# Attention of a two-block network: the value products of a pair in one turn instead of two

## The reference

```python
def gqa_attend(q, k, v):
    bsz, nq, _, _ = q.shape
    qg = q.reshape(bsz, nq, KV_HEADS, ATT_HEADS // KV_HEADS, HEAD_DIM)
    s = jnp.einsum('bqhgd,bkhd->bhgqk', qg, k).astype(jnp.float32) * HEAD_DIM ** -0.5
    p = jax.nn.softmax(s, axis=-1).astype(v.dtype)
    o = jnp.einsum('bhgqk,bkhd->bqhgd', p, v)
    return o.reshape(bsz, nq, ATT_HEADS * HEAD_DIM)
...
    k_all = jnp.concatenate([kc, kx], axis=1)
    v_all = jnp.concatenate([vc, vx], axis=1)
    o_x = lax.map(lambda qb: gqa_attend(qb, k_all, v_all), q_blocks)
    y_x = o_x.swapaxes(0, 1).reshape(bsz, n, nq) @ w_out
```

## Time and profile before

| | |
|---|---|
| median of 3 runs | 2515.29 us (2514.77 to 2516.95) |
| profiled execution: span from first to last instruction | 2512.5 us; the median lies 2.8 us above it, and no other time of this execution is given |
| PE busy | 2491.2 us, 99% |
| DVE busy | 1611.4 us, 64% |
| ACT busy | 972.5 us, 39% |
| mean granted TensorE clock | 0.998 |

### The profile page before, as it was taken

One profiled execution on the slowest core, in us unless ns is written; L12 is line 12 of the kernel. 1 busy time (PEld: TensorE's weight loads), 2 busy tenths in 40 slices (PEclk: granted clock), 3 DMA queues, 4 the chain that ended last, 5 costly groups with the idle time before them and its releaser, 6 DMA issues.

```text
span 2512.5 us, 36307 instructions
## 1 busy us (share of the span) xinstructions
PE 2491.2 (99%) x14058; PEld 2125.8 (85%) x14058; DVE 1611.4 (64%) x2551; ACT 972.5 (39%) x1483; POOL 117.9 (5%) x211
## 2 busy tenths in 40 slices
PE   8999999999999999999999999999999999999998
PEld 6888888888888888779888888898888888888887
DVE  5777667665546567766655575776667777644446
ACT  6243533131313245764332244353232454533224
POOL 0000000100000000000000000010001000000000
PEclk9999999999999999999999999999999999999999
DMA  7323314433333321002545553224546323132222
GB/s 288 120 99 110 127 50 143 159 118 110 114 110 134 110 76 51 2 1 93 199 152 169 173 192 113 101 88 172 187 158 219 135 95 110 68 101 93 100 96 97
DMA packets 83965, 303.70 MB, mean 121 GB/s; under 512 B 9200, under 2 KB 11376, under 8 KB 83568
## 3 DMA queue, kind: packets, MB, share of 16 engines
q1 hardware_dynamic: 58336, 208.92, 24.0%
q0 software_dynamic: 25488, 92.81, 10.8%
HBM read 299.60 MB, written 2.10 MB: 120 GB/s over the span
## 4 chain that ended last, share of the span: by engine, by line
PE 96%; DMA 2%; DVE 1%; issue 0%; ACT 0%; SPq 0%; POOL 0%; POOLq 0%; ACTq 0%; DVEq 0%
PE G L648 20%; PE G L650 20%; PE G L649 20%; PE G L675 5%; PE G L676 5%; PE G L677 5%; PE G L742 2%; PE G L743 2%; PE G L744 2%; PE B L1243 2%; PE G L827 1%; DMA Araw<-adaw_dram 1%; PE G L829 1%; PE G L828 1%; PE B L1219 1%; PE G L1203 1%
## 5 line engine op out<-in xcount | busy, mean ns | idle before, releaser
L1391 ACT ACTIVATE Whi<-Wraw 128x1024 fp32r<-128x1024 f32 x333 | 349.6, 1051 | 411.4 <-DMA Wraw<-wstream_dram 399.3
L2038 DVE TENSOR_TENSOR Wlo<-Wraw,Whi 128x1024 fp32r<-128x1024 f32 x333 | 406.9, 1222 | 116.4 <-ACT Whi L1391 115.2
L648 PE MATMUL G<-hs_hi,Whi 128*128 128x512 f32 x672 | 264.2, 393 | 0.0
L650 PE MATMUL G<-hs_hi,Wlo 128*128 128x512 f32 x672 | 261.6, 389 | 0.0
L649 PE MATMUL G<-hs_lo,Whi 128*128 128x512 f32 x672 | 261.5, 389 | 0.0
L2053 DVE SCALAR_TENSOR_TENSOR Araw<-Araw,CB 128x1024 f32<-128x1024 f32 x176 | 214.3, 1220 | 20.6 <-DMA Araw<-adaw_dram 20.5
L2113 DVE SCALAR_TENSOR_TENSOR X<-G,MOD,X 128x256 f32<-128x256 f32 (+1 forms) x104 | 65.2, 655 | 206.0 <-PE G L650 154.9
L594 POOL DMA_DIRECT2D Araw<-adaw_dram x176 | 93.2, 530 | 1692.4 <-DVE Araw L2053 1637.9
L648 PE MATMUL G<-h_lat_hi,Whi 128*128 128x512 f32 x424 | 165.7, 391 | 0.0
L649 PE MATMUL G<-h_lat_lo,Whi 128*128 128x512 f32 x424 | 165.1, 389 | 0.0
L650 PE MATMUL G<-h_lat_hi,Wlo 128*128 128x512 f32 x424 | 165.1, 389 | 0.0
(11 more groups left out here) (636 smaller groups left out, 6169.5 us busy)
## 6 DMA issues: line engine op xcount, KB each, us to landing
Wraw<-wstream_dram SPq DMA_DIRECT2D x333, 512.0 KB, 3.3
Araw<-adaw_dram POOLq DMA_DIRECT2D x176, 512.0 KB, 3.8
Eraw<-wstream_dram SPq DMA_DIRECT2D x22, 512.0 KB, 4.4
FIRST<-firstw_dram SPq DMA_DIRECT2D x6, 1024.0 KB, 18.7
X<-xin_dram SPq DMA_DIRECT2D x4, 768.0 KB, 7.0
X<-xin_dram SPq DMA_DIRECT2D x2, 1536.0 KB, 7.3
out_dram<-X SPq DMA_DIRECT2D x16, 128.0 KB, 1.7
ROW<-rows_dram SPq DMA_DIRECT2D x2, 768.0 KB, 6.5
```

Of the source, the lines that this page charges most:

```text
L648: pe.matmul(o, wh, hi[:, a:b], start=(k == 0), stop=False)
L650: last = pe.matmul(o, wl, hi[:, a:b], start=False, stop=(k == kt - 1))
L1391: act.activation(hi, raw, ACT.Copy).then_inc(w_hi, 1)
L2038: dve.tensor_tensor(lo, raw, hi.bitcast(F32), ALU.subtract).then_inc(w_lo, 1)
```

## The change

PE's list in the attention is written in another order. In even turns from 2 on all six key tiles are done for the pair; odd turns have no values; the exception of the last turn is gone. ACT's and DVE's lists stay as they are, and so do all waits.

```diff
@@ -1268,8 +1268,7 @@
             scores_of(0)
             latent_values(1, 2, 3, 4)
             for n in range(2 * AH):
-                r, i0 = n // 2 - 1, 3 * (n % 2)
-                last_pair = n + 1 == 2 * AH
+                r = n // 2 - 1
                 if n == 2:
                     pe.wait_ge(qk_std, 4)
                     pe.wait_ge(at_used_act, 3)
@@ -1280,12 +1279,10 @@
                     latent_values(7)
                 for part in range(3):
                     turn_probs(n, part)
-                    if last_pair and part == 0:
-                        attend(r, i0)
                 if n == 0:
                     latent_values(5, 6)
-                if r >= 0:
-                    for i in range(i0 + 1 if last_pair else i0, i0 + 3):
+                if r >= 0 and n % 2 == 0:
+                    for i in range(TT):
                         attend(r, i)
                 if n % 4 == 0 and n > 0:
                     spread_sums(n // 4 - 1)
```

## The result

The changed kernel takes 2532.45 us (median of 5 runs, 2530.26 to 2532.91), the kernel before 2514.77 us beside it (5 runs, 2512.66 to 2516.95): 17.7 us more, ratio 1.007, 95% interval 1.0059 to 1.008. The forecast was 2533.5 us, 18.2 us more than the 2515.3 us known then.

A forecast was written before the change was run, and what follows sets the result against it. PE was taken to bound the kernel, with the chain on it for 96% of the span. 20.0 - 0.3 - 0.8 - 0.7 = +18.2 us on 2515.3 gave 2533.5 us, range 2530.5 to 2538.5.

The forecast's parts named there:

- Odd turns: Odd turns 3 to 29: without values, scores wait for the first head's exponential, 2.90 us after the transposes; -0.3 us.
- Even turns: Even turns 2 to 30: six more value matmuls each, paid in full at 1.33 us, +20.0 us in all.
- The sums' copy: Turns 4, 8, ... 28: longer values cover the transposes' wait for ACT's copy of the sums; 7 x -0.12 = -0.8 us.
- The end: Turn 31's transposes to the spread: 5.04 us instead of 5.75, with a new 0.9 us wait for DVE's copy; -0.7 us.
- the reason for the wait: Scores in odd turns: held by the first head's exponential, whose accumulator read ends 2.80 us after the transposes start.
- the second exponential 0.2 us ahead: Second head's exponential: ends 0.2 us before the next transposes' second piece wants it, and that stays.
- the hidden wait (1): Odd turns: scores could start right behind the transposes, so no slower, 2513.8 us; chance 0.05.
- The additional wait (2): Behind odd turns: transposes' second piece waits too, or scores pay a weight load; +3 us, 2536.5 us; chance 0.09.
- The clock (3): PE's idle time in odd turns lowers its clock to 1.2 GHz: 2571 us, or 2657 for the whole stretch; chance 0.02.

The follow-up runs named there:

- odd_left_out: The kernel before with the six value matmuls of each odd turn 3 to 29 left out: 2515.62 us against 2514.8, ratio 1.0003.
- even_twice: The kernel before with the three key tiles of every even turn 2 to 30 multiplied twice: 2534.21 us against 2514.8, ratio 1.0075.
- exp_first: The changed kernel with ACT doing the first head's exponential ahead of its two copies from turn 2 on: 2552.16 us against 2514.92 before, ratio 1.0141.
- no_second_copy: The changed kernel without ACT's copy of the second piece of transposed probabilities from turn 4 on: 2531.2 us against 2514.92 before, ratio 1.0062.
- mirror: The changed kernel with all six key tiles in the odd turns and none in the even ones: 2534.78 us against 2514.8 before, ratio 1.0075.
- exp_first_split: The kernel before, values in every turn, with ACT's first exponential ahead of its two copies: 2531.12 us against 2514.7, ratio 1.0061.

## Why the prediction was right

By its steps, with the stretch's +17.25 us:

- **Odd turns, -0.3 us.** Right: the scores wait for the exponential. Measured 2.85 us after the transposes, against 2.91 in some turns and 2.88 in those behind a spread: -0.06 us in 7 turns, -0.03 us in 7, together -0.6 us, twice the forecast and near the lower bound. The step missed it by taking ACT's start, 0.77 us after the transposes, as fixed; it became 0.69 (why, the last section says). odd_left_out gives the whole value of 84 matmuls as 0.4 us.
- **Even turns, +20.0 us.** Right in kind, 0.6 us too large: twelve records more cost 2.64 - 1.35 = 1.29 us a turn, not 1.33, together 19.4 us. even_twice pays the same 1.29 us for added work.
- **The sums' copy, -0.8 us.** Right: scores to transposes 1068.35 - 1067.10 = 1.25 us instead of 1.36.
- **The end, -0.7 us.** Right to 0.03 us: 5.01 us instead of 5.75, with 0.88 us of wait for DVE where 0.9 was expected.
- Sum of the measured terms: 19.4 - 0.6 - 0.8 - 0.7 = 17.3 us, against 17.25 measured. The forecast of 18.2 us is 1 us above it by the first two terms.

That the profiled span came out at the forecast 2530.7 us to the digit is luck. The stretch grew 1 us less than forecast, and outside it 1 us was added, about which the forecast said nothing: the attention started 2.2 us later, mostly by the early dip of the clock, and 1.2 us went behind it.

What the prediction had incomplete is the reason for the wait. It named only the exponential, since it comes last, at 2.80 us; the scores also need ACT's two copies and DVE's. exp_first shows that this matters as soon as someone tries to repair the wait by ACT's order. It was also right to call the second exponential 0.2 us ahead, but it drew nothing from it; no_second_copy shows that this is the next limit.

Of the rivals, the hidden wait (1) is refuted by the idle rows and by odd_left_out. The additional wait (2) did not appear in the changed kernel. The clock (3) stayed at 1.00 in the stretch. The Trainium skill's sentence on transposes (page "TensorE: Matmul & The Clock Gate", Part 4), by which the emptied turns were at risk, made no difference at 1.32 us of idle time: the granted clock was 1.00. In exp_first, with 2.07 us behind the transposes, the clock did fall; whether the kind of matmul has a part in that, and not only the idle time, was not tested.

## What to carry to other kernels

An engine that is busy 99% of the time can still have work that costs nothing. Before moving work away from between two instructions, add up the other engines' chain between them: here the way from the transposes through copies and exponential to the start of the next scores takes 2.85 us, and the work between fitted it to 0.06 us, so work taken out there turned into waiting and work put in elsewhere was paid in full. And a wait on several semaphores has to be read as several chains: shortening the last one brings out the one behind it.

## What the runs showed of the hardware

- Idle time and the clock. With PE idle for 1.32 us every second turn (changed kernel), 1.32 to 1.39 us (odd_left_out), 1.38 and 0.9 us (mirror) or 0.6 us in most turns (exp_first_split) the granted clock stayed at 1.00 over the stretch. With 2.07 us every second turn (exp_first) it was 0.93, in seven falls to 1.2 GHz that cost 1.5 to 1.6 us each. Length of one idle time, idle time altogether and the turns without values change together from run to run, so which of them decides stays open.
- The clock also dipped with PE busy for 10.00 of 10.00 us by the profile, at 80 to 90 us of the span: 0.83 in the changed kernel, 0.74 to 0.85 in the profiled executions of the eight experiments. That of before alone has no dip there. The cause is open. A difference of some 2 us between two whole spans can come from that, so terms of 0.5 us were read from the stretch and not from the medians.
- The 0.06 us that odd turns gained. ACT starts its first copy 0.69 us after the transposes in turn 15 of the changed kernel, where it had been idle for 1.12 us. In turn 15 of before it was 0.77 us, and ACT was not idle there but came to the copy of the earlier trace rows straight from a half of the output:

```profile
1047.51 0.62 ACT L1918 ACTIVATE ao_hi<-Junk 128x512 fp32r<-128x512 f32 x1
```

In the changed kernel this piece of work is over before the transposes begin (1056.88 + 0.62 = 1057.50, transposes at 1057.93), since the longer even turn leaves ACT time for it. In odd_left_out it is as late as before (in turn 15 at 1050.60, the copy at 1051.12, 0.76 us after the transposes), and in its turns 7, 11, ... 27 the scores come after 2.90 to 2.92 us: nothing gained. That kernel's 0.4 us come from the turns behind a spread, where the scores come after 2.82 us in place of 2.88, and from turn 3.
